# Operand addresses 64 bytes below the weight tiles modulo 256, and the first network's tanh in PSUM

## The reference, cut to what matters

```python
for l in range(DEPTH):                       # DEPTH = 2
    # h = modulated rmsnorm(x)
    # p = h @ w_in: a gated convolution branch, a windowed attention branch, two gates
    # x += g * (gated sum of the two branches) @ w_out
    # h2 = modulated rmsnorm(x)
    # up: h2 @ w_up (2 x 2816 columns), a three-tap convolution over the tokens,
    #     a * silu(g), then  @ w_down;   x += g2 * that
```

## Time and profile before

| | us |
|---|---|
| median of 3 runs | 1959.35 (1958.83 to 1960.12) |
| the profiled execution, from its first to its last instruction | 1959.9 |
| TensorE clock granted, mean | 0.994 of full |

### The profile page before, as it was taken

One profiled execution on the slowest core, in us unless ns is written; L12 is line 12 of the kernel. 1 busy time (PEld: TensorE's weight loads), 2 busy tenths in 40 slices (PEclk: granted clock), 3 DMA queues, 4 the chain that ended last, 5 costly groups with the idle time before them and its releaser, 6 DMA issues.

```text
span 1959.9 us, 33261 instructions
## 1 busy us (share of the span) xinstructions
PE 1904.2 (97%) x12126; PEld 1624.1 (83%) x12126; DVE 1065.5 (54%) x1972; ACT 891.8 (46%) x1520; POOL 1187.7 (61%) x904
## 2 busy tenths in 40 slices
PE   7999999999999999999899999999999999999998
PEld 4677777888888887877889999787999998769987
DVE  4899865354443324887657744876542048555400
ACT  4223444243443323525546645556554355555533
POOL 2444233424654554635469987674788876649986
PEclk9999999999999999999999999999999999999999
DMA  9942233628433343436465575432455564326554
GB/s 387 362 127 76 56 96 117 228 78 172 147 107 107 120 149 121 150 91 211 139 204 172 182 230 182 164 108 89 130 183 182 173 206 139 109 75 205 185 179 130
DMA packets 121541, 307.04 MB, mean 157 GB/s; under 512 B 29640, under 2 KB 51528, under 8 KB 121044
## 3 DMA queue, kind: packets, MB, share of 16 engines
q1 hardware_dynamic: 118808, 300.98, 46.8%
q10 hardware_dynamic: 2620, 4.51, 1.5%
HBM read 300.72 MB, written 8.06 MB: 158 GB/s over the span
## 4 chain that ended last, share of the span: by engine, by line
issue 36%; POOL 31%; PE 28%; DVE 4%; ACT 1%; POOLq 0%; ACTq 0%; DVEq 0%
POOL w_lo L803 30%; PE bank L1369 7%; PE bank L1374 6%; PE bank L1370 6%; PE bank L2081 2%; PE bank L2082 2%; PE bank L2083 2%; DVE nb L2258 1%; PE bank L1966 1%; PE bank L1968 1%; PE bank L1967 1%; ACT w_hi L846 0%; DVE v_lo L2258 0%; PE bank L2185 0%; DVE v_lo L2250 0%
## 5 line engine op out<-in xcount | busy, mean ns | idle before, releaser
L803 POOL TENSOR_TENSOR w_lo<-raw,w_hi 128x512 fp32r<-128x512 f32 x884 | 1169.7, 1353 | 759.4 <-ACT w_hi L846 757.2
L846 ACT ACTIVATE w_hi<-raw 128x1024 fp32r<-128x1024 f32 x442 | 466.1, 1056 | 285.2 <-PE bank L1374 146.8
L1369 PE MATMUL bank<-h_hi,w_hi 128*128 128x256 f32 (+1 forms) x1248 | 407.4, 342 | 1.8 <-DVE h_lo L2258 1.1
L1370 PE MATMUL bank<-h_lo,w_hi 128*128 128x256 f32 (+1 forms) x1248 | 399.4, 336 | 0.0
L1369 PEld LDWEIGHTS bank<-h_hi,w_hi 128*128 128x128 f32 x1248 | 237.2, 190 | 43.0 <-issue 13.2
L1374 PE MATMUL bank<-h_hi,w_lo 128*128 128x256 f32 (+1 forms) x1248 | 262.8, 335 | 0.0
L1370 PEld LDWEIGHTS bank<-h_lo,w_hi 128*128 128x128 f32 x1248 | 237.3, 190 | 23.6 <-issue 0.2
L1374 PEld LDWEIGHTS bank<-h_hi,w_lo 128*128 128x128 f32 x1248 | 204.7, 190 | 23.9
L1369 PE MATMUL bank<-u_hi,w_hi 128*128 128x272 f32 (+1 forms) x736 | 212.0, 288 | 1.1 <-DVE u_lo L2258 1.1
L1374 PE MATMUL bank<-u_hi,w_lo 128*128 128x272 f32 (+1 forms) x736 | 209.1, 284 | 0.0
L1370 PE MATMUL bank<-u_lo,w_hi 128*128 128x272 f32 (+1 forms) x736 | 208.3, 283 | 0.0
(11 more groups left out here) (394 smaller groups left out, 3720.8 us busy)
## 6 DMA issues: line engine op xcount, KB each, us to landing
raw<-in_wstream SPq DMA_DIRECT2D x442, 512.0 KB, 3.5
ada_raw<-in_wada SPq DMA_DIRECT2D x48, 512.0 KB, 13.1
late_a<-in_wada SPq DMA_DIRECT2D x16, 512.0 KB, 5.1
late_b<-in_wada SPq DMA_DIRECT2D x16, 512.0 KB, 4.5
biash<-rpb_by_offset SPq DMA_DIRECT2D x64, 64.0 KB, 2.5
gates<-in_wada SPq DMA_DIRECT2D x8, 512.0 KB, 5.0
rpb_by_offset<-in_rpb SPq DMA_DIRECT2D x16, 224.0 KB
bias_by_distance<-vec ACTq DMA_DIRECT2D x1, 3264.0 KB
```

Source lines behind the costliest of these rows:

```text
L803: i = pool.tensor_tensor(lo[:, part, s, :], whole[:, part, :], hi[:, part, s, :].bitcast(F32), ALU.subtract)
L846: act.activation(w_hi[q >= first["l2", 0]][:, :, s, :], raw[:, s, :].rearrange("p (g c) -> p g c", c=PAIR), ACT.Copy)\
L1369: pe.matmul(o, tile(w_hi, i, k), a_hi, start=start, stop=False)
L1370: pe.matmul(o, tile(w_hi, i, k), a_lo, start=False, stop=False)
```

## The change

It does four things.

- `h_*`, and with it everything placed behind it (`gates`, `qT`, `kT`, `V`, `upad`, `cv`), starts 64 bytes below the weight tiles modulo 256; `cv` and the second network's `o_*` get a padding of their own to that place. The shifted second views of the attention and convolution branches go, and the offsets of `fa_*`, `u_*`, `f_*` are rewritten so that they stand modulo 256 where they stood. `dn_*` stays at offset 0.
- A constant table of 128x128 that nothing reads (`ones_h`) goes.
- The tanh of up is written to banks 4 and 5 in turn instead of `up_t`. For j = 1 of the first layer ACT first waits for `vec_ready`, which frees bank 5.
- Because banks 4 and 5 are in use till the end of up, the early groups of down fill banks 0, 1, 6, 7, and wait until block j = 20 is through: `up_out` at 21 in the first layer, `up_split` at 21 in the second. The weights of those groups are packed to match.

```diff
-DOWN_ORDER = [(range(0, 2), range(4, DC)), *pairs(2, 6)[2:], (range(0, 2), range(0, 4)), *pairs(2, 6)[:2],
+DOWN_EARLY, DOWN_LATER = (0, 1, 6, 7), (2, 3, 4, 5)
+DOWN_ORDER = [(range(0, 2), DOWN_EARLY), *pairs(2, 6)[0::3], (range(0, 2), DOWN_LATER), *pairs(2, 6)[1:3],
               *pairs(14, FF_C), *pairs(6, 14)]
...
+        def up_turned(j):
+
+            return aux[j % 2]
...
         X = sb("X", [DC, T_BOTH])
+        top[0] += (w_at - 64 - top[0]) % 256
         h_at = top[0]
...
-        fa_hi = at("fa_hi", [FF_C, SEQ], F32R, g_at + 192)
-        fa_lo = at("fa_lo", [FF_C, SEQ], F32R, g_at + 192 + FF_C * SEQ * 4)
+        fa_hi = at("fa_hi", [FF_C, SEQ], F32R, g_at)
+        fa_lo = at("fa_lo", [FF_C, SEQ], F32R, g_at + FF_C * SEQ * 4)
...
-        top[0] += (128 - top[0]) % 256
+        top[0] += (w_at - 64 - top[0]) % 256
         cv_at = top[0]
...
-        attns = [(at_hi, at_lo), (shifted("as_hi", QC, q_at, 192), shifted("as_lo", QC, q_at + QC * T_BOTH * 4, 192))]
-        convs = [(cv_hi, cv_lo), (shifted("cs_hi", CONV_C, up_at, 192), shifted("cs_lo", CONV_C, cv_at, 192))]
...
-                    act.activation(up_t[:, b % 2, 0:T], up_g[:, b % 2, 0:T], ACT.Tanh)\
+                    if (layer, j) == (0, 1) and it is None:
+                        act.wait_ge(*after("vec_ready", 0))
+                    act.activation(up_turned(b)[:, 0:T], up_g[:, b % 2, 0:T], ACT.Tanh)\
...
                 if layer == 0:
-                    down(0, range(4, DC))
-                    down(1, range(4, DC))
+                    pe.wait_ge(sem("up_out"), FF_C - 1)
+                    down(0, DOWN_EARLY)
+                    down(1, DOWN_EARLY)
...
-                        if n < 3:
-                            pe.wait_ge(sem("up_split"), js[-1] + 1)
+                        if n == 0:
+                            pe.wait_ge(sem("up_split"), FF_C - 1)
...
-                    t_ = up_t[:, b % 2, 0:T]
+                    t_ = up_turned(b)[:, 0:T]
```

More of the change, by code:

```diff
@@ L113 @@
 _n = 0
-for _name, _w in (("ident", P), ("ones_d", P), ("ones_c", P), ("ones_h", P), ("perm1", P), ("perm2", P),
+for _name, _w in (("ident", P), ("ones_d", P), ("ones_c", P), ("perm1", P), ("perm2", P),
                   ("sel", 8), ("hsel", 16), ("sums", 2), ("cos1", SEQ), ("sin1", SEQ), ("win", GRID_W),
@@ L306, in build @@
         ffn_mid = [tuple(at(f"f_{part}{l}", [FF2_C, n_mid], F32R, o + by + n * FF2_C * n_mid * 4) for n, part in enumerate(("hi", "lo")))
-                   for l, (n_mid, by) in enumerate(((T2, 192), (SEQ, 0)))]
+                   for l, (n_mid, by) in enumerate(((T2, 0), (SEQ, 64)))]
         o += (L2_FRONT * T2 + 3 * 1024) * 4
+        o += (w_at - 64 - o) % 256
         o_hi = at("o_hi", [DC, T2], F32R, o)
@@ L342, in build @@
         ident = cst[:, 0:P]
[L343 to L346, removed]
+        ones_d, ones_c = (cst[:, i * P:(i + 1) * P] for i in (1, 2))
+        perm1, perm2, sel = cst[:, 3 * P:4 * P], cst[:, 4 * P:5 * P], cst[:, 5 * P:5 * P + 8]
+        hsel = cst[:, 5 * P + 8:5 * P + 24]
+        sums = cst[:, 5 * P + 24:5 * P + 26]
         by_distance = nc.dram_tensor("bias_by_distance", (A_HEADS + B_HEADS, P, VLEN), F32).ap()
@@ L991, in attend @@
                         act.wait_ge(*after("attn_pv", (layer, n)))
-                        copy(attns[layer][0][:, n, 0:T], aux[3][:, 0:T]).then_inc(*done("attn_hi", (layer, n)))
+                        copy(at_hi[:, n, 0:T], aux[3][:, 0:T]).then_inc(*done("attn_hi", (layer, n)))
                     elif kind == "var":
@@ L1708, in attention_branch @@
                     for k in range(4):
-                        three(bank[m % 4][:, 0:T], s + m, 4 + k, attns[layer][0][:, k, 0:T], attns[layer][1][:, k, 0:T], k == 0, k == 3)
+                        three(bank[m % 4][:, 0:T], s + m, 4 + k, at_hi[:, k, 0:T], at_lo[:, k, 0:T], k == 0, k == 3)
                 def conv_branch(m):
@@ L1716, in conv_branch @@
                             pe.wait_ge(*after("conv_lo", (layer, k)))
-                        mm = three(bank[b][:, 0:T], s + m, k, convs[layer][0][:, k, 0:T], convs[layer][1][:, k, 0:T], k == 0, k == 3)
+                        mm = three(bank[b][:, 0:T], s + m, k, cv_hi[:, k, 0:T], cv_lo[:, k, 0:T], k == 0, k == 3)
                     mm.then_inc(*done("slab_used", s + m))
@@ L1830, in network1 @@
                 if layer == 0:
-                    down(0, range(4, DC))
-                    down(1, range(4, DC))
+                    pe.wait_ge(sem("up_out"), FF_C - 1)
+                    down(0, DOWN_EARLY)
+                    down(1, DOWN_EARLY)
                     pe.wait_ge(*after("up_all", layer))
-                    down(0, range(4)).then_inc(*done("slab_used", s))
-                    down(1, range(4)).then_inc(*done("slab_used", s + 1))
+                    down(0, DOWN_LATER).then_inc(*done("slab_used", s))
+                    down(1, DOWN_LATER).then_inc(*done("slab_used", s + 1))
                     for j in range(2, 4):
@@ L3103, in blocks @@
         for js, ms in order:
-            slabs.append(np.concatenate([chunks[j, :, ms[0] * P:(ms[-1] + 1) * P] for j in js], axis=1))
+            slabs.append(np.concatenate([chunks[j, :, m * P:(m + 1) * P] for j in js for m in ms], axis=1))
     for l in range(DEPTH):
```

19 lines of the change are left out of this document (8 added, 11 removed).

## The result

The changed kernel takes 1963.36 us in the median of 20 runs, the kernel before 1959.96 (20 runs beside them); the ratio is 1.0018, with a 95% interval of 1.0011 to 1.0025. So it is 3.4 us slower where 23.6 us of gain were forecast. Of the forecast's rivals D, with its 1962.9 us, lies nearest.

A forecast was written before the change was run, and what follows sets the result against it. PE's matmul pace was taken as the bound, with an address-dependent stall. 4320 moved matmuls at 6.6 ns gain 28.5 us, less 4.6 in attention and 0.3 waiting: 23.6 gained, 1935.7 us against the median; range 1928.5 to 1950.

The forecast's parts named there:

- D: 512-column products at -64: one more stall per matmul, 6.6 ns on 2208, 14.6 us lost; 1962.9 us, chance 0.05.
- The price at 512 columns: 2208 moved 512-column matmuls: 6.6 ns gained each, 14.6 us; bounds a gain of 6.7 ns and nothing.
- The price at 256 columns: 2112 moved 256-column matmuls: from 120.0 to 113.3 ns each, 13.9 us gained.
- What is given back in the attention: Attention of both layers: 29 slabs' gain lost where PE waits for partners, 4.6 us; bounds none and 7.1.
- The tanh: Up's tanh in PSUM: nothing by itself; layer 1's two reading steps fall from 1.53 and 1.40 to about 0.4 us.
- the wait ahead of down: PE before down: nothing in layer 0, 0.3 us lost in layer 1 waiting for block 20's split; bounds 0 and 2.5.
- POOL: Up of layer 1: POOL needs 2.59 us a slab against PE's 2.72, so no new wait.
- C: Address is not the cause; h keeps 120.0 and 226.7 ns: 1959.6 us, chance 0.06.

The follow-up runs named there:

- the turns only: The kernel before with only the tanh in PSUM, the new early down groups and their waits, every address kept: 1957.42 us, ratio 0.9985.
- by width: Kernel with only the tanh and down changes, plus second-layer h and y shifted by 192 bytes, first layer at offset 0: 1948.94 us, ratio 0.9944.
- the addresses alone: The changed kernel with the tanh back in up_t and the old down groups and waits: 1968.76 us, ratio 1.0052.

## Why the prediction was wrong

**The price at 512 columns, the step that failed.** The prediction bounded the 2208 matmuls by "a gain of 6.7, if the stall is the same one (as the equal 13.3 left over at both widths says), and nothing". The lower bound had no reason behind it: no row excluded a loss, and the same text had a rival whose mechanism was one. Measured: +6.7 ns, 226.7 to 233.3. Of the 2208 matmuls 2112 lie in layer 0 and would cost 2112 x 6.7 = 14.2 us; 10.8 show. The missing 3.4 us lie ahead of up, where PE and DVE wait for each other, as part of a gain would have. The forecast had -14.6 in this place, so this one sign makes most of the 27 us between forecast and result. The equal 13.3 at two widths were taken as evidence of one stall that keeps its price when the place changes; they only said that at offset 0 the width does not matter.

**The price at 256 columns, a size taken too large.** "Two sets of rows show both ends" was right for the end before, 120.0. The end after, 113.3, was read from the attention, convolution and `fa` of one execution, and these had all fallen into the better of two paces; with the turns only, at the same addresses, `fa` ran at 117.8. In the changed kernel the 256 columns of layer 0 ran at 113.3, but `y` and all of up of layer 1 behind its first 96 matmuls at 117.8. Up of layer 1 won 2.8 us where 7 were forecast; by width, at 113.4, it won 6.4, so the arithmetic was sound and the pace was not. There was a row that spoke: the second network's 272 columns at offset -64, which the prediction read as 123.8 ns. Read as the windows are read here they had (94.00 + 0.29) / 759 = 124.2, which is 10.9 over the columns' time, close to the 11.1 of the slower pace. The prediction put that down to the stride. That it was the slower pace is argued here, not shown: single distances there run from 120 to 128 ns.

**What is given back in the attention** cannot be checked as it stood, since the gain was not there. Layer 1 up to `up` changed by -0.7 and +2.2 us in the two profiles.

**The tanh and the wait ahead of down** held: 0.43 us a step, no wait where 0.3 was taken. The prediction gave the steps no value by themselves, since they run beside PE. At the old pace that holds: with the turns only, up of layer 1 takes 127.8 us, as before. With the addresses alone PE waited 1.0 us for `fa_lo`; most of the 5.4 us by which that kernel's median lies above the changed one's is not accounted for by it.

**POOL** kept up, as argued: even at 113.4 ns up of layer 1 shows PE busy for 90.00 of 90.00 us.

**The rivals.** D had the sign (a loss at 512 columns), its price and its point of decision: `h`, `y`, attention and convolution all pay, more than its 1680 matmuls. Its reason, a stream longer than the weight load, no run shows. It came out half a microsecond beside the median, by some luck: the gain at 256 columns was smaller than it took, layer 0 lost less, and the second network scatters by more than that. At a chance of 0.05 it was held far too unlikely; "for it" stood the one row at -64 that did not show the full gain. C is excluded by the tables above: moving the weight tiles alone changes the pace. By the Trainium skill, TensorE: Matmul & The Clock Gate, section Back-to-back issue gap, the distance is N / 2.4 + 2.5 ns for an isolated matmul, and at large N the section has a stream of weight loads and matmuls go faster than that. The traces here disagree with both: no steady stretch of the first network, at any place and width, came under N / 2.4 + 6.7 (113.3 ns at 256 columns).

## What to carry to other kernels

Where the rows show an effect at one width only, its price at another width has two signs until a row or a reason excludes one; a term that is half the sum and has no row must not be bounded by "gain or nothing". A pace read from a single execution may be one of several: profile the same kernel twice before multiplying it by thousands of matmuls. And place the moved operand by the width it streams: here at the weight tile's own place modulo 256 for 512 columns, 64 bytes to either side of it for 256.

## What the hardware showed that was not expected

- The distance of fp32r matmuls depends on the place of the moved operand against the weight tile modulo 256 bytes, and with the opposite sign at the two widths: 226.7 to 233.3 ns at 512 columns from 0 to -64, 120.0 to 113.3 or 117.8 at 256.
- Over three matmuls (the group of one product) what is left above the columns' time is 3, 5, 6, 7 or 9 times 6.7 ns (the time of 16 columns) at offsets 0, -64 and +64: 113.3, 117.8, 120.0 and 226.7, 228.9 and 233.3 ns a matmul. It is not a whole number of them at +128 (232.4 at 512 columns), -96 (118.7 at 256) and -32 (118.3 at 256). Why is open: no run shows the mechanism.
- At -64 and 256 columns there are two paces that hold for as long as nothing interrupts PE (958 matmuls in a row at either), and +64 showed both as well. With an 8-column matmul ahead of each block the pace went to and fro over 20 blocks without exception; at PE's own waits it changed at five of nine.
